# Query and key projection of a two-layer mixer: from full-precision tiles to pieces of high and low parts

## The chip, the cores and the metric

The kernel runs on one core of a Trainium2 chip. The metric is the device time of one execution in microseconds (us). One core has a matrix engine (PE, with its weight loads listed as PEld), a vector engine (DVE), a scalar engine (ACT), a general engine (POOL), and SyncE (SP), which here only issues transfers. Each engine works through its own list in order; an instruction that waits for a semaphore holds up everything behind it on that engine. On-chip memory is SBUF (128 partitions) and PSUM, eight banks of 128 x 512 words into which PE accumulates.

## What is computed

Two trunk layers over 384 tokens: 128 context tokens and 256 latent ones. Each layer projects the normalised tokens once and hands the columns to three groups:

```python
u = h @ p['w_in']                      # 1024 -> 512 + 768 + 1536 columns
y_a = conformer_group(u_a, p)          # gated, 31-tap depthwise convolution, layer norm, silu
y_b = hyena_group(u_b, p)              # two long convolutions, by spectra
q, k, v = jnp.split(u_c, 3, axis=-1)   # 512 columns each
if ang is not None:
    q = apply_axial_rope(q, ang)       # latent tokens only
    k = apply_axial_rope(k, ang)
k_all = jnp.concatenate([ctx_kv[0].astype(k.dtype), k], axis=2)   # cached keys first
o = diff_attention(q, k_all, v_all, lam)
y = jnp.concatenate([y_a, y_b, o], axis=-1) @ p['w_out']
```

After that comes a mixture of 64 experts, eight per token. All tensors are 32-bit floats.

## The kernel before

Everything is written out by hand: five engine programs, semaphores between them, and every buffer placed by hand, some over others. There is no scheduler. What orders the work is the order of each engine's list.

**The projection** of a layer is 19 tiles, which PE runs in a loop over `i` (in `block.tensor`). Tiles 0 to 9 are 128 output columns by 384 tokens, for the convolution groups. Tiles 10 to 18 are 128 tokens by 512 columns: 10 to 12 are the query's three token tiles, 13 to 15 the key's, 16 to 18 the value's. The semaphore `pe_u` counts finished tiles. Each tile goes to one of three PSUM banks, and `u_free` makes it wait until the tile three before it was read out (`u_out`, on ACT).

**Two ways of multiplying.** `u_tile` multiplies the 32-bit operands as they are; the trace records two instructions for each such product. Tiles 2 to 9 (`HALVED`) instead go by single passes: a weight piece of 128 x 1024 is rounded to a high part by ACT (`high`), its remainder, the low part, is written over the original by DVE for pieces 0 and 1 and by POOL for 2 to 7 (`RINGL` is the same memory as `RING`), and PE adds three products: high x high, low x high, high x low. The tokens are split once per layer into `HTH` and `HTL`. The high parts rotate through three buffers, two in `GROWH` and `SCRH`, so ACT's cast of one piece waits until PE has done with the piece that held the buffer (`act.wait_ge(pe_u, ...)`).

**Between the tiles** PE runs the long convolution of the hyena group, in two rounds: `z_turn` (6 transposes), `z_spectra` (18 products), and `z_conv` (12 products); each needs something from ACT or DVE in between. DVE's list in this stretch is: `gated`, `taps(0, 4)`, `z_spectra` of round 0, `taps(4, 16)`, `z_gate` of round 0, `rope` of the query, `taps(16, 24)`, `z_spectra` of round 1, `taps(24, 31)`, `conv_bias`, `rope` of the key, `z_gate` of round 1. A tap is a `scalar_tensor_tensor` over 399 columns that reads two SBUF operands, `CB` and `CA`; there are two per tap, and each waits only for the one before the last, so they run without a gap. PE's `conv_mean` waits for `conv_bias`, its `z_turn` of round 1 for `z_gate` of round 0.

**Placement** that matters: `HTH` lies under `YT`, `HTL` under the end of `KSYS`, `QT` and the first half of `KT`. `rope` keeps its four products in `RP`, which is the second half of `YT`.

**Transfers**: SP loads the query chunk `t0` after tile 3, the key chunk `t1` after tile 5, the value chunk `t2` after tile 9, then the cached keys `ck` into `KT`, and later pieces of the modulation weights and `w_out` into the slots that come free.

Of the kernel before, what the change touches and what calls it, by code (L numbers as in the profile page):

```python
# [28 lines left out]
P = 128  # L29
DM = 1024  # L30
KD = DM // P
DEPTH = 2
NT = 3
# [15 lines left out]
CHW = 4096  # L49
# [52 lines left out]
def build(nc, I, O):  # L102
    lam_init = [0.8 - 0.6 * math.exp(-0.3 * l) for l in range(DEPTH)]
    with ExitStack() as ctx:
# [12 lines left out]
        with ExitStack() as o_RINGL:  # L117
            RINGL = sb("RINGL", [P, SLOTS * CHW], F32R, c=o_RINGL)
        RING = sb("RING", [P, SLOTS * CHW])
# [122 lines left out]
        M2 = RWF[:, 1280:1792].rearrange("p (a n) -> p a n", a=2)  # L242
        ON = RWF[:, 1792:2048].rearrange("p (b n) -> p b n", b=2)

        RP = YT[:, 4:8, :].rearrange("p a b -> p (a b)")
        XN = (YT[:, :, :].rearrange("p a b -> p (a b)").rearrange("p (t d) -> p t d", t=NT),
              FLT[:, 0:NT * DM].rearrange("p (t d) -> p t d", t=NT))
        XNK = [x.rearrange("p t (q k) -> p t k q", k=KD) for x in XN]
        WHI = [GROWH[:, 0, :], GROWH[:, 1, :], SCRH[:, :]]
        HALVED = tuple(range(2, 10))  # L250
        NH3 = len(HALVED)
        FTB = ((0, 2, 4), (6, 0, 2))
        ROWB = (6, 6, 4, 6)
        COLB = (6, 5, 4, 5)
# [83 lines left out]
             "d_rope", "d_ln", "d_zs", "d_gate", "d_max", "d_P", "d_oms", "d_on", "d_x", "d_rt",  # L338
             "d_res", "d_lam"))

        a_hh, a_wh, d_hl, d_wl, p_wl = map(sem, ("a_hh", "a_wh", "d_hl", "d_wl", "p_wl"))
        p_half, p_pad, p_pow = map(sem, ("p_half", "p_pad", "p_pow"))


# [50 lines left out]

        def split_piece(l, q):

            n = ORDER[HALVED[q]]
            a, count = SLOT_OF[l, f"f{n // 4}"]
            cols = slice(a * CHW + (n % 4) * DM, a * CHW + (n % 4 + 1) * DM)  # L400
            return a, count, RING[:, cols], RINGL[:, cols], WHI[q % 3]

        HTHF = HTH[:, :, :].rearrange("p k t -> p (k t)")
        HTLF = HTL[:, :, :].rearrange("p k t -> p (k t)")
# [5 lines left out]
        def _(sp):  # L410
# [7 lines left out]
            def weight_in(l, name):  # L418

                a = SLOT_OF[l, name][0]  # L420
                if name[0] == "f":
                    i = int(name[1])
                    src = I["wfm"][l, :, i * CHW:min((i + 1) * CHW, 10 * DM)]
                elif name[0] == "t":
                    src = I["wtm"][l, int(name[1])]
                else:
                    src = I["wo"][l, int(name[1])]
                sp.dma_start(chunk[a][:, 0:src.shape[-1]], src).then_inc(chunk_in[a], 16)

            def tiles_done(l, n):  # L430
                sp.wait_ge(pe_u, 19 * l + n)
# [16 lines left out]
            for l in range(DEPTH):  # L448
# [21 lines left out]
                weight_in(l, "t1")  # L470
                tiles_done(l, 10)
                weight_in(l, "t2")
                sp.dma_start(KT[:, :, P:2 * P], I["ck"][l]).then_inc(ctx_in, 16)
                tiles_done(l, 13)
                mod_in(fill(l, 0)[0])
                tiles_done(l, 16)
                weight_in(l, "o0")
                sp.wait_ge(pe_conv, 4 * (l + 1))
                mod_in(fill(l, 1)[0])
# [171 lines left out]
        def _(pe):  # L651
# [72 lines left out]
            def z_turn(l, o):  # L724

                if o == 0:
                    pe.wait_ge(a_spec, 6 * l + 6)
                    pe.wait_ge(d_sc, K_SC * l + 12)
                else:
                    pe.wait_ge(d_gate, K_GATE * l + 4)  # L730
                for t in range(NT):
                    for c in range(2):
                        mm = nc.tensor.transpose(PS[t // 2][:, (t % 2) * 256 + c * P:(t % 2) * 256 + (c + 1) * P],
                                                 CO[:, c, t * P:(t + 1) * P], ident)
                mm.then_inc(pe_ztr, 1)
# [162 lines left out]
            def u_rest(l, i):  # L898
# [6 lines left out]
                    mm = nc.tensor.matmul(PS[3 + i % 3][:, 0:TOK], hi[:, k, :], HTL[:, k, :], start=False, stop=(k == KD - 1))  # L905
                mm.then_inc(pe_u, 1)

            def u_tile(l, i):

                n = ORDER[i]  # L910
                name = f"f{n // 4}" if n < 10 else f"t{(n - 10) // 3}"
                a, count = SLOT_OF[l, name]
                pe.wait_ge(chunk_in[a], 16 * count)
                u_free(l, i)
                if n < 10:
                    w = RING[:, a * CHW + (n % 4) * DM:a * CHW + (n % 4 + 1) * DM].rearrange("p (k f) -> p k f", k=KD)
                    for k in range(KD):
                        mm = nc.tensor.matmul(PS[3 + i % 3][:, 0:TOK], w[:, k, :], HT[:, k, :], start=(k == 0), stop=(k == KD - 1))  # L918
                else:
                    w = RING[:, a * CHW:(a + 1) * CHW].rearrange("p (k n) -> p k n", k=KD)  # L920
                    t = (n - 10) % 3
                    for k in range(KD):
                        mm = nc.tensor.matmul(PS[3 + i % 3][:, :], HT[:, k, t * P:(t + 1) * P], w[:, k, :],  # L923
                                              start=(k == 0), stop=(k == KD - 1))
                mm.then_inc(pe_u, 1)
# [223 lines left out]
            for l in range(DEPTH):  # L1149
# [15 lines left out]
                        to_features(l, 0, t)  # L1165

                features_done(l, 0, 2)
                for i in range(19):
                    if i not in HALVED:
                        u_tile(l, i)  # L1170
                    elif i == 2:
                        u_high(l, 2)
                        u_high(l, 3)
                        u_rest(l, 2)
                        u_rest(l, 3)
                    elif i > 3:
                        u_high(l, i)
                        u_rest(l, i)
                    if l > 0 and i < 2:
                        hidden(l, i)  # L1180
                    if 3 <= i < 6:
                        filters(l, i - 3)
                    if 6 <= i < 9:
                        spectra(l, i - 6)
                    if i in (9, 13):
                        z_turn(l, i // 10)
                    if i in (10, 14):
                        z_spectra(l, i // 13)
                    if i in (12, 16):
                        z_conv(l, i // 15)  # L1190
                    if i == 16:
                        conv_mean(l)
                    if i == 17:
                        conv_var(l)
                    if i >= 17:
                        for h in range(NH):
                            qk_turn(l, i - 17, h)
# [91 lines left out]
        def _(act):  # L1289
# [141 lines left out]
            def z_out(l, o):  # L1431
                act.wait_ge(pe_ztr, 2 * l + o + 1)
                if o == 0:
                    act.wait_ge(d_sc, K_SC * l + 12)
                own.sig(sc.activation(ZT[:, 0:2, :].rearrange("p t n -> p (t n)"), PS[0][:, :], ACT.Copy), a_zt)
                own.sig(sc.activation(ZT[:, 2, :], PS[1][:, 0:256], ACT.Copy), a_zt)

            def high(l, q):

                a, count, whole, low, high_ = split_piece(l, q)  # L1440
                act.wait_ge(chunk_in[a], 16 * count)
                if q == 0:
                    act.wait_ge(d_x, 6 * l)
                    act.wait_ge(pe_mod, 1)
                if q >= 3:
                    act.wait_ge(pe_u, 19 * l + HALVED[q - 3] + 1)
                sc.activation(high_, whole, ACT.Copy).then_inc(a_wh, 1)

            def u_out(l, i):
# [25 lines left out]
            for l in range(DEPTH):  # L1475
# [29 lines left out]
                high(l, 1)  # L1505

                act.wait_ge(p_pad, 6 * (l + 1))
                for i in range(19):
                    u_out(l, i)
                    if l > 0 and i < 2:  # L1510
                        hidden(l, i)
                    if 1 <= i < 7:
                        high(l, i + 1)
                    if 6 <= i < 9:
                        spectra(l, i - 6)
                    if i in (9, 13):
                        z_out(l, i // 10)
                    if i >= 17:
                        for h in range(NH):
                            qk_out(l, i - 17, h)  # L1520
# [67 lines left out]
        def _(dve):  # L1588
# [318 lines left out]

            def rope(l, c):

                for t in (1, 2):  # L1910
                    dve.wait_ge(a_u, K_AU * l + au(10 + 3 * c + t))
                    x = QKV[:, t, 512 * c:512 * (c + 1)].rearrange("p (g h s i) -> p g h s i", g=8, h=2, s=2)
                    x1, x2 = x[:, :, :, 0, :], x[:, :, :, 1, :]
                    cs = cst("cos")[:, (t - 1) * 32:t * 32].rearrange("p (h i) -> p h i", h=2).unsqueeze(1).to_broadcast([P, 8, 2, 16])
                    sn = cst("sin")[:, (t - 1) * 32:t * 32].rearrange("p (h i) -> p h i", h=2).unsqueeze(1).to_broadcast([P, 8, 2, 16])
                    T = [RP[:, j * 256:(j + 1) * 256].rearrange("p (g h i) -> p g h i", g=8, h=2) for j in range(4)]
                    own.wait(d_rope)
                    sig(v.tensor_tensor(T[0], x1, cs, ALU.mult), d_rope)
                    sig(v.tensor_tensor(T[1], x2, sn, ALU.mult), d_rope)
                    sig(v.tensor_tensor(T[2], x1, sn, ALU.mult), d_rope)  # L1920
                    sig(v.tensor_tensor(T[3], x2, cs, ALU.mult), d_rope)
                    own.wait(d_rope)
                    sig(v.tensor_tensor(x1, T[0], T[1], ALU.subtract), d_rope)
                    sig(v.tensor_tensor(x2, T[2], T[3], ALU.add), d_rope)
# [306 lines left out]
```

## Time and profile before

| | us |
|---|---|
| median of 3 runs (1756.74 to 1760.15) | 1758.61 |
| profiled execution | 1757.6 |
| its span in the trace | 1755.8 |
| PE busy, share of the span | 1666.8, 95% |
| DVE busy | 644.9, 37% |
| ACT busy | 387.0, 22% |
| POOL busy | 220.8, 13% |
| granted PE clock, mean | 0.978 |

The share of PE is an average over stages. Which engine sets the pace of one stage is seen from the idle time in that stage alone. The stretch that the change touches begins, in layer 0, at 107.5 us with `z_turn` and ends at 195.4 us with the first attention product; layer 1 has the same stretch 860.2 us later. In a row, a name such as `RING` is a buffer, and `PSB` the whole of PSUM.

### The profile page before, as it was taken

How to read it: one execution, taken by the hardware profiler on the slowest of the kernel's cores; microseconds unless marked ns; L12 is line 12 of the kernel's file. 1: busy time of each engine (PE TensorE's matmuls, PEld its weight loads, DVE VectorE, ACT ScalarE, POOL GpSimd, SP SyncE). 2: the span in 40 equal slices, each digit the busy share in tenths (PEclk: the TensorE clock that was granted, in tenths of full speed). 3: DMA queues.
4: the chain of work that ended last, by engine and by line, in shares of the span. 5: the costliest groups of instructions: out<-in, count | busy, mean ns of one | idle time of the engine just before them, and what ended most of it. 6: DMA issues, size and time to landing. Idle time of an engine off the chain costs nothing.

```text
span 1755.8 us, 22346 instructions
## 1 busy us (share of the span) xinstructions
PE 1666.8 (95%) x8468; PEld 823.9 (47%) x8468; DVE 644.9 (37%) x1709; ACT 387.0 (22%) x842; POOL 220.8 (13%) x217
## 2 busy tenths in 40 slices
PE   4999889999999999999969998999999999999996
PEld 2765344644444444444447553555444444444442
DVE  2479362422222222222165866442222222222223
ACT  2310343211111111111153114431111111111111
POOL 0200000011111111111103000001111111111110
PEclk8999999999999999999979998999999999999998
DMA  9312744399999999999732229017899999999993
GB/s 402 131 54 100 281 207 174 126 403 373 417 400 418 416 394 413 421 419 419 322 127 96 102 96 395 1 60 316 341 418 411 408 419 393 414 419 419 420 419 126
DMA packets 77291, 530.52 MB, mean 302 GB/s; under 512 B 10880, under 2 KB 14080, under 8 KB 21632
## 3 DMA queue, kind: packets, MB, share of 16 engines
q1 hardware_dynamic: 67392, 503.90, 70.3%
q0 software_dynamic: 9792, 25.18, 3.7%
q8 instruction: 69, 1.13, 0.3%
q14 instruction: 38, 0.31, 0.0%
HBM read 533.76 MB, written 5.77 MB: 307 GB/s over the span
## 4 chain that ended last, share of the span: by engine, by line
PE 90%; DVE 4%; DMA 2%; ACT 2%; issue 1%; SPq 0%; ACTq 0%; POOL 0%; DVEq 0%
PE PSB L931 30%; PE PSB L940 15%; PE PSB L923 7%; PE PSB L985 6%; PE PSB L986 5%; PE PSB L973 4%; PE PSB L859 4%; DMA RING<-in_wmod 2%; PE PSB L679 1%; PE PSB L918 1%; PE PSB L895 1%; PE PSB L958 1%; PE PSB L905 1%; PE PSB L896 1%; PE PSB L947 1%
## 5 line engine op out<-in xcount | busy, mean ns | idle before, releaser
L931 PE MATMUL PSB<-WB,EX 128*32 128x512 f32 (+2 forms) x1408 | 431.9, 598 | 0.0
L931 PE MATMUL PSB<-RING,EX 128*32 128x512 f32 (+2 forms) x1344 | 417.1, 598 | 1.7 <-DVE EX L1770 1.7
L940 PE MATMUL PSB<-RING,AT 128*32 128x512 f32 (+2 forms) x720 | 226.7, 597 | 4.8 <-ACT GROW L1298 3.7
L1788 DVE TENSOR_TENSOR YL<-PSB,YH 128x512 fp32r<-128x512 f32 x136 | 94.1, 692 | 353.7 <-ACT YH L1377 353.7
L940 PE MATMUL PSB<-WB,AT 128*32 128x512 f32 (+2 forms) x704 | 210.8, 596 | 0.0
L563 POOL TENSOR_SCALAR SCAT<-CST,LSTT 128x384 fp32r<-128x384 f32 x68 | 84.9, 1248 | 833.1 <-PE PSB L986 833.0
L931 PEld LDWEIGHTS PSB<-WB,EX 128*32 128x32 f32 (+2 forms) x1408 | 113.0, 126 | 135.7 <-issue 135.7
L985 PE MATMUL PSB<-YH,SCAT 128*128 128x512 f32 x408 | 171.7, 421 | 2.8 <-DVE YL L1788 2.8
L931 PEld LDWEIGHTS PSB<-RING,EX 128*32 128x32 f32 (+2 forms) x1344 | 105.8, 124 | 122.5 <-issue 122.5
L1770 DVE COPY EX<-PSB 128x512 f32<-128x512 f32 x68 | 47.1, 692 | 315.7 <-PE PSB L973 315.7
L986 PE MATMUL PSB<-YL,SCAT 128*128 128x512 f32 x408 | 161.0, 395 | 0.0
L1377 ACT ACTIVATE YH<-PSB 128x512 fp32r<-128x512 f32 x136 | 81.2, 597 | 239.6 <-PE PSB L940 239.6
L923 PE MATMUL PSB<-RING,HT 128*128 128x512 f32 x288 | 125.9, 592 | 0.0
L973 PEld LDWEIGHTS PSB<-CST,XG 128*128 128x128 f32 x544 | 58.5, 141 | 106.6 <-issue 104.8
L940 PEld LDWEIGHTS PSB<-RING,AT 128*32 128x32 f32 (+2 forms) x720 | 62.5, 129 | 78.1 <-issue 74.2
L1370 ACT ACTIVATE SGM<-PSB 128x256 f32<-128x256 f32 x68 | 26.1, 383 | 311.9 <-PE PSB L931 311.9
L940 PEld LDWEIGHTS PSB<-WB,AT 128*32 128x32 f32 (+2 forms) x704 | 58.4, 126 | 72.5 <-issue 72.0
L973 PE MATMUL PSB<-CST,XG 128*128 128x128 f32 x544 | 88.2, 285 | 1.4 <-ACT EX L1352 1.4
L555 POOL DMA_INDIRECT XG<-h_rows,IDX x68 | 74.5, 1096 | 113.4 <-DVE LSTW L1740 91.2
L985 PEld LDWEIGHTS PSB<-YH,SCAT 128*128 128x128 f32 x408 | 77.6, 190 | 21.1 <-issue 4.9
L859 PE MATMUL PSB<-RING,YT 128*128 128x512 f32 x192 | 86.5, 598 | 0.0
L923 PEld LDWEIGHTS PSB<-RING,HT 128*128 128x128 f32 x288 | 54.3, 190 | 63.0 <-issue 62.2
(282 smaller groups left out, 1867.9 us busy)
## 6 DMA issues: line engine op xcount, KB each, us to landing
RING<-in_exp_w_gate SPq DMA_DIRECT2D x64, 1024.0 KB, 12.3
RING<-in_exp_w_up SPq DMA_DIRECT2D x64, 1024.0 KB, 14.4
RING<-in_exp_w_down SPq DMA_DIRECT2D x64, 1024.0 KB, 12.8
WB<-in_exp_w_gate SPq DMA_DIRECT2D x64, 1024.0 KB, 10.1
WB<-in_exp_w_up SPq DMA_DIRECT2D x64, 1024.0 KB, 13.6
WB<-in_exp_w_down SPq DMA_DIRECT2D x64, 1024.0 KB, 13.3
RING<-in_wmod SPq DMA_DIRECT2D x16, 2048.0 KB, 10.4
KSYS<-in_wmod SPq DMA_DIRECT2D x8, 2048.0 KB, 11.6
```

The costliest lines, as they stand in the source:

```text
L555: pool.indirect_dma_start(XG[:, s % 2, :], None, h_rows, bass.IndirectOffsetOnAxis(ap=IDX[:, s:s + 1], axis=0), bounds_check=TOK - 1, oob_ ...
L563: nc.gpsimd.tensor_scalar(SCAT[:, s % 2, :], cst("iota"), LSTT[:, s:s + 1], None, ALU.is_equal).then_inc(p_scat, 1)
L859: mm = nc.tensor.matmul(PS[YB[0][t] + hf][:, :], YT[:, f, t * P:(t + 1) * P], w[:, f, :], start=(f == 0), stop=(f == 7))
L923: mm = nc.tensor.matmul(PS[3 + i % 3][:, :], HT[:, k, t * P:(t + 1) * P], w[:, k, :], start=(k == 0), stop=(k == KD - 1))
L931: mm = nc.tensor.matmul(PS[6][s0:s0 + w, :].rearrange("p (w f) -> p w f", w=2), e[:, k, s0:s0 + w], rawgu[n % NBUF][:, k], start=(k == 0), ...
L940: mm = nc.tensor.matmul(dst[s0:s0 + w, :], AT[:, j, s0:s0 + w], rawdn[n % NBUF][:, hf, j], start=(j == 0), stop=(j == 1))
L973: mm = nc.tensor.transpose(PS[7][:, c * P:(c + 1) * P], XG[:, s % 2, k * P:(k + 1) * P], ident)
L985: nc.tensor.matmul(PS[piece][:, :], w, YHb[s % 2][:, cols], start=False, stop=False, skip_group_check=True)
L986: mm = nc.tensor.matmul(PS[piece][:, :], w, YLb[s % 2][:, cols], start=False, stop=True, skip_group_check=True)
L1377: sc.activation(YHb[s % 2][:, hf * 512:(hf + 1) * 512], PS[6 + hf][:, :], ACT.Copy).then_inc(a_yh, 1)
L1770: v.tensor_copy(EX2[:, s % 2, 4:8, :].rearrange("p k s -> p (k s)"), PS[7][:, :]).then_inc(e_high, 1)
L1788: v.tensor_tensor(YLb[s % 2][:, hf * 512:(hf + 1) * 512], PS[6 + hf][:, :], YHb[s % 2][:, hf * 512:(hf + 1) * 512].bitcast(F32), ALU.subtr ...
```

## The change

The query and key tiles (10 to 15) leave `u_tile`. Each of their two chunks (128 x 4096 weights) is cut into four pieces of two contraction blocks, 128 x 1024 each. ACT rounds a piece to its high part, POOL writes the low part over the original, and PE (`qk_piece`) takes the piece for all three token tiles at once: for two blocks and three tiles, three products each, 18 in all. So a chunk's three tiles stay open in three banks and are finished in its last piece. The eight new pieces use only the two `GROWH` buffers in turn; ACT's cast waits for the piece two before it, by the new semaphore `pe_wk` (or `pe_u` at the end of a chunk).

PE's list is written out again around them: `z_turn` 0, piece 0, `z_spectra` 0, pieces 1 to 3, `z_conv` 0, piece 4, `z_turn` 1, piece 5, `z_spectra` 1, pieces 6 and 7, then the value tiles as before. ACT's and POOL's lists get the casts and the subtractions. DVE's list keeps its order. `RP` moves from `YT` to `SCR` (over `SCRH`), and `rope` waits for tile 7. Since `HTH` and `HTL` now live until tile 15, the cached keys, which land over `HTL`, are loaded after tile 15 instead of behind `t2`.

```diff
-        RP = YT[:, 4:8, :].rearrange("p a b -> p (a b)")
+        RP = SCR[:, 0:DM]
-        NH3 = len(HALVED)
+        NFM, NH3 = len(HALVED), len(HALVED) + 8
         def split_piece(l, q):
+            if q < NFM:
+                n = ORDER[HALVED[q]]
+                name, part, high = f"f{n // 4}", n % 4, WHI[q % 3]
+            else:
+                c, part = divmod(q - NFM, 4)
+                name, high = f"t{c}", WHI[q % 2]
...
-                sp.dma_start(KT[:, :, P:2 * P], I["ck"][l]).then_inc(ctx_in, 16)
                 tiles_done(l, 13)
                 mod_in(fill(l, 0)[0])
                 tiles_done(l, 16)
+                sp.dma_start(KT[:, :, P:2 * P], I["ck"][l]).then_inc(ctx_in, 16)
                 weight_in(l, "o0")
...
+            def qk_piece(l, c, j):
+                q = NFM + 4 * c + j
+                a, count, whole, low, high = split_piece(l, q)
+                pe.wait_ge(p_wl, (NH3 - 2) * l + q - 1)
+                hi = high.rearrange("p (k n) -> p k n", k=2)
+                lo = low.rearrange("p (k n) -> p k n", k=2)
+                for kk in range(2):
+                    k = 2 * j + kk
+                    for t in range(NT):
+                        i = 10 + 3 * c + t
+                        if k == 0:
+                            u_free(l, i)
+                        dst = PS[3 + i % 3][:, :]
+                        ht, hl = HTH[:, k, t * P:(t + 1) * P], HTL[:, k, t * P:(t + 1) * P]
+                        nc.tensor.matmul(dst, ht, hi[:, kk, :], start=(k == 0), stop=False)
+                        nc.tensor.matmul(dst, ht, lo[:, kk, :], start=False, stop=False)
+                        mm = nc.tensor.matmul(dst, hl, hi[:, kk, :], start=False, stop=(k == KD - 1))
+                        if k == KD - 1:
+                            mm.then_inc(pe_u, 1)
+                if j < 3:
+                    mm.then_inc(pe_wk, 1)
...
-                if q >= 3:
+                if 3 <= q < NFM:
                     act.wait_ge(pe_u, 19 * l + HALVED[q - 3] + 1)
+                elif NFM <= q < NFM + 2:
+                    act.wait_ge(pe_u, 19 * l + HALVED[q - 2] + 1)
+                elif q == NFM + 5:
+                    act.wait_ge(pe_u, 19 * l + 13)
+                elif q >= NFM + 2:
+                    act.wait_ge(pe_wk, 6 * l + q - NFM - 1 - (1 if q > NFM + 5 else 0))
                 sc.activation(high_, whole, ACT.Copy).then_inc(a_wh, 1)
...
             def rope(l, c):
+                dve.wait_ge(pe_u, 19 * l + 8)
```

PE in layer 0 before, from the first transposes of the long convolution (L733) to its spectra (L745, L749) and the query tiles (L923, each row of one and seven is a tile):

```order
L733 MATMUL PSB<-CST,CO 128x128 [waits d_sc,a_spec]
L733 MATMUL PSB<-CST,CO 128x128 x5
L923 MATMUL PSB<-RING,HT 128x512 [waits a_u,chunk_in0]
L923 MATMUL PSB<-RING,HT 128x512 x7
L745 MATMUL PSB<-RW,CST 128x256 [waits a_zt]
L745 MATMUL PSB<-RW,CST 128x256
L749 MATMUL PSB<-RW,CST 128x256 x8
L923 MATMUL PSB<-RING,HT 128x512 [waits d_u,chunk_in0]
```

PE at the same place in the change; L738 is the transposes, L750 and L754 the spectra, L928 to L930 the three products of one block and token tile:

```order
L738 MATMUL PSB<-CST,CO 128x128 [waits d_sc,a_spec]
L738 MATMUL PSB<-CST,CO 128x128 x5
L928 MATMUL PSB<-GROWH,HTH 128x512 [waits a_u,p_wl]
L929 MATMUL PSB<-RINGL,HTH 128x512
L930 MATMUL PSB<-GROWH,HTL 128x512
...
L750 MATMUL PSB<-RW,CST 128x256 [waits a_zt]
L750 MATMUL PSB<-RW,CST 128x256
L754 MATMUL PSB<-RW,CST 128x256 x8
L928 MATMUL PSB<-GROWH,HTH 128x512 [waits p_wl]
```

A tile's wait for its chunk (`chunk_in0`) has become a piece's wait for POOL's low part (`p_wl`), and one piece stands between the transposes and the spectra where a whole tile stood.

ACT before, from the sigmoid of tile 9 (L1457) over the read-outs of `z_turn` (L1435, L1436) and of the projection tiles (L1463):

```order
L1457 ACTIVATE SG<-PSB 128x384 [waits pe_u]
L1435 ACTIVATE RW<-PSB 128x512 [waits d_sc,pe_ztr]
L1436 ACTIVATE RW<-PSB 128x256
L1463 ACTIVATE QKV<-PSB 128x512 [waits pe_u] x4
L1435 ACTIVATE RW<-PSB 128x512 [waits pe_ztr]
L1436 ACTIVATE RW<-PSB 128x256
```

ACT in the change, with the casts to the high part as L1492 and the read-outs as L1474, L1475 and L1508:

```order
L1492 ACTIVATE GROWH<-RING 128x1024 [waits pe_u,chunk_in0]
L1502 ACTIVATE SG<-PSB 128x384 [waits pe_u]
L1474 ACTIVATE RW<-PSB 128x512 [waits d_sc,pe_ztr]
L1475 ACTIVATE RW<-PSB 128x256
L1492 ACTIVATE GROWH<-RING 128x1024 [waits pe_u,chunk_in0]
L1492 ACTIVATE GROWH<-RING 128x1024 [waits pe_wk,chunk_in0] x2
L1492 ACTIVATE GROWH<-RING 128x1024 [waits pe_wk,chunk_in2]
L1508 ACTIVATE QKV<-PSB 128x512 [waits pe_u] x3
L1492 ACTIVATE GROWH<-RING 128x1024 [waits pe_u,chunk_in2]
L1474 ACTIVATE RW<-PSB 128x512 [waits pe_ztr]
L1475 ACTIVATE RW<-PSB 128x256
L1492 ACTIVATE GROWH<-RING 128x1024 [waits pe_wk,chunk_in2] x2
```

The eight casts stand among the read-outs, and the second `z_turn` is read out between the sixth and the seventh of them.

## Rows read from the trace of the kernel before

**Rows 1.** Windows, both layers: length; busy of PE, PEld, DVE, ACT, POOL; clock.

```profile
107.50:195.00 87.50, 86.44 (x286) 48.59 (x283) 62.81 (x127) 10.98 (x26) 0.86 (x1) 1.00 0.28 103
968.00:1055.00 87.00, 86.16 (x284) 48.34 (x281) 62.82 (x127) 10.70 (x25) 0.86 (x1) 1.00 0.28 103
```

**Rows 2.** Timeline of PE in that stretch, layer 0: start, length, operation, count.

```profile
108.18 7.03 PE L923 MATMUL PSB<-RING,HT 128*128 128x512 f32 x16
115.05 1.03 PE L745 MATMUL PSB<-RW,CST 128*128 128x256 f32 x4
...
119.36 13.90 PE L923 MATMUL PSB<-RING,HT 128*128 128x512 f32 x32
133.09 0.61 PE L759 MATMUL PSB<-CST,KSYS 128*128 128x128 f32 x4
...
137.44 7.03 PE L923 MATMUL PSB<-RING,HT 128*128 128x512 f32 x16
...
174.23 1.45 PE L772 MATMUL PSB<-CB,CST 128*128 128x384 f32 x4
```

**Rows 3.** Timeline of PE in an expert step: single-pass products of 512 columns.

```profile
414.28 0.40 PE L986 MATMUL PSB<-YL,SCAT 128*128 128x512 f32 x1
...
415.66 0.40 PE L986 MATMUL PSB<-YL,SCAT 128*128 128x512 f32 x1
```

**Rows 4.** Timeline of ACT, one cast, and line L633, POOL's subtractions: min/median/max ns.

```profile
66.71 1.06 ACT L1447 ACTIVATE GROWH<-RING 128x1024 fp32r<-128x1024 f32 x1
...
L633 POOL TENSOR_TENSOR RINGL<-RING,GROWH x8: 2360/2397/3828, 67.8 to 948.0; 128x1024 fp32r<-128x1024 f32 x8
```

**Rows 5.** Timelines of DVE and POOL around 70 us, layer 0.

```profile
69.65 0.69 DVE L1856 TENSOR_TENSOR QKV<-PSB,CST 128x512 f32<-128x512 f32 x1 [15.67 <-PE PSB L702]
70.97 2.15 DVE L1858 TENSOR_TENSOR QKV<-QKV 128x512 f32<-128x512 f32 x1
...
67.85 4.72 POOL L633 TENSOR_TENSOR RINGL<-RING,GROWH 128x1024 fp32r<-128x1024 f32 x2 [4.52 <-ACT GROWH L1447]
```

**Rows 6.** Timelines of DVE and POOL around 88 us, and POOL's twin in layer 1.

```profile
86.62 2.72 DVE L1876 SCALAR_TENSOR_TENSOR CO<-RW,PR,CO 128x128 f32<-128x128 f32 x8
89.38 3.20 DVE L1873 TENSOR_SCALAR CO<-RW,PR 128x128 f32<-128x128 f32 x4
...
87.76 3.83 POOL L633 TENSOR_TENSOR RINGL<-RING,GROWH 128x1024 fp32r<-128x1024 f32 x1 [3.50 <-ACT GROWH L1447]
...
947.97 3.83 POOL L633 TENSOR_TENSOR RINGL<-RING,GROWH 128x1024 fp32r<-128x1024 f32 x1 [3.50 <-ACT GROWH L1447]
```

**Rows 7.** Timeline of DVE in the touched stretch, layer 0.

```profile
116.11 0.69 DVE L1945 TENSOR_TENSOR RW<-PSB,KSYS 128x512 f32<-128x512 f32 x1 [3.10 <-PE PSB L745]
...
122.48 13.17 DVE L1898 SCALAR_TENSOR_TENSOR CA<-CB,PR,CA 128x399 f32<-128x399 f32 x24
...
137.64 0.61 DVE L1956 SCALAR_TENSOR_TENSOR CO<-CO,PR,PSB 128x384 f32<-128x384 f32 x1 [0.87 <-PE PSB L764]
...
143.36 8.81 DVE L1898 SCALAR_TENSOR_TENSOR CA<-CB,PR,CA 128x399 f32<-128x399 f32 x16
...
167.02 1.03 DVE L1905 TENSOR_TENSOR CB<-CA,PR 128x256 f32<-128x256 f32 x2
```

**Rows 8.** Timeline of PE and windows of 1 us behind a pause, attention of layer 0.

```profile
228.79 0.55 PE L1220 MATMUL PSB<-CST,HT 128*128 128x128 f32 x3 [2.00 <-DVE HT L2064]
...
229.00:230.00 1.00, 1.00 (x7) 0.30 (x9) 0.90 (x4) 0.54 (x2) 0.55 (x1) 0.66 0.96 410
230.00:231.00 1.00, 1.00 (x12) 0.24 (x8) 0.93 (x3) 0.95 (x3) 0.00 (x0) 0.50 0.97 410
231.00:232.00 1.00, 1.00 (x12) 0.18 (x4) 0.93 (x3) 0.86 (x3) 0.00 (x0) 0.50 1.11 475
232.00:233.00 1.00, 1.00 (x9) 0.19 (x2) 1.00 (x1) 0.04 (x1) 0.00 (x0) 0.64 0.95 393
```

**Rows 9.** Transfers: KB each, median us from issue to landing.

```profile
KT<-in_ck SPq DMA_DIRECT2D x2, 256.0 KB, 8.3
```

More of the change, by code:

```diff
@@ L339, in build @@
              "d_res", "d_lam"))
-        a_hh, a_wh, d_hl, d_wl, p_wl = map(sem, ("a_hh", "a_wh", "d_hl", "d_wl", "p_wl"))
+        a_hh, a_wh, d_hl, d_wl, p_wl, pe_wk = map(sem, ("a_hh", "a_wh", "d_hl", "d_wl", "p_wl", "pe_wk"))
         p_half, p_pad, p_pow = map(sem, ("p_half", "p_pad", "p_pow"))
@@ L396, in split_piece @@
         def split_piece(l, q):
[L398 to L401, printed above, removed]
+            if q < NFM:
[4 more added lines that the diff above has]
+                name, high = f"t{c}", WHI[q % 2]
+            a, count = SLOT_OF[l, name]
+            cols = slice(a * CHW + part * DM, a * CHW + (part + 1) * DM)
+            return a, count, RING[:, cols], RINGL[:, cols], high
         HTHF = HTH[:, :, :].rearrange("p k t -> p (k t)")
@@ L1167, in _ @@
                 features_done(l, 0, 2)
-                for i in range(19):
+                for i in range(10):
                     if i not in HALVED:
@@ L1184, in _ @@
                         spectra(l, i - 6)
[L1185 to L1190, printed above, removed]
+                z_turn(l, 0)
+                qk_piece(l, 0, 0)
+                z_spectra(l, 0)
+                qk_piece(l, 0, 1)
+                qk_piece(l, 0, 2)
+                qk_piece(l, 0, 3)
+                z_conv(l, 0)
+                qk_piece(l, 1, 0)
+                z_turn(l, 1)
+                qk_piece(l, 1, 1)
+                z_spectra(l, 1)
+                qk_piece(l, 1, 2)
+                qk_piece(l, 1, 3)
+                for i in range(16, 19):
+                    u_tile(l, i)
+                    if i == 16:
+                        z_conv(l, 1)
                     if i == 16:
@@ L1507, in _ @@
                 act.wait_ge(p_pad, 6 * (l + 1))
-                for i in range(19):
+                for i in range(10):
                     u_out(l, i)
@@ L1515, in _ @@
                         spectra(l, i - 6)
-                    if i in (9, 13):
-                        z_out(l, i // 10)
+                    if i == 8:
+                        high(l, 8)
+                z_out(l, 0)
+                for q in range(9, 13):
+                    high(l, q)
+                for i in range(10, 13):
+                    u_out(l, i)
+                high(l, 13)
+                z_out(l, 1)
+                high(l, 14)
+                high(l, 15)
+                for i in range(13, 19):
+                    u_out(l, i)
                     if i >= 17:
```

## The prediction

> **What bounds the kernel now.** I read the windows first. In the touched stretch PE is busy for 86.4 of 87.5 us at full clock, in both layers, and POOL does next to nothing there (0.86 us) [rows 1]. DVE is busy for 62.8 us. So PE sets the pace, and work taken off PE counts in full as long as nothing else gets in front. Then the timeline of PE, for what a tile and each piece of the long convolution cost [rows 2]; then the timelines of ACT, POOL and DVE, for what the new pieces will wait for [rows 4 to 7]. The sum is made against the profiled execution (1757.6 us, of which 1755.8 are the span); it lies 1.0 us below the median of the runs.
>
> **PE's own work.** Two query tiles take 13.73 us (119.36 to 133.09) [rows 2], so a tile takes 6.87 and six take 41.2. The new form has 8 pieces of 18 single-pass products. In the expert step such a product of 512 columns starts every 0.23 us (415.66 less 414.28, over six) [rows 3], so a piece takes 4.14 and eight take 33.1: **8.1 us less per layer**. The cast on ACT is 1.06 us, POOL's subtraction 2.40 [rows 4]; eight of each are 8.5 and 19.2 us per layer, on engines that are busy for 11.0 and 0.9 us in the stretch [rows 1]. By this count alone a piece's preparation (0.2 us from PE to ACT, 1.06, 0.1, 2.40, 0.1: 3.9 us) just fits behind one piece of PE, and POOL would hide it.
>
> **What POOL's subtraction meets.** It does not run freely beside DVE. At 70.97 a DVE operation with two SBUF operands, whose equal behind it took 0.68, took 2.15 and ended 0.55 after POOL's; one with a PSUM operand at 69.65 took its usual 0.69 under POOL [rows 5]. The other way round: at 87.76 POOL's subtraction was released while DVE was 1.1 us into a run of eight `scalar_tensor_tensor` of two SBUF operands. It took 3.83 instead of 2.40, that is 1.43 more, and ended at 91.59, so its own 2.40 began at 89.19, just where that run ended (86.62 + 2.72); the run lost nothing, and DVE's next group of four took 3.20. Layer 1 repeats it to the hundredth [rows 6]. So POOL does not get in between two such instructions while the run goes on; it waits for the run's end, and then DVE waits for POOL.
>
> The Trainium skill (SBUF — State Buffer, section "Who interferes with whom") says that a DVE instruction with two SBUF inputs contends with a GpSimd instruction that reads SBUF, and that whoever issues first has the shared ports for that whole instruction while the other fully blocks. For POOL behind DVE the rule read by itself would let POOL in after one instruction of about 0.55 us, which would make the first rival below, 1769, out of what I forecast as 1780; the trace agrees with the blocking (2.15 for 0.68) and shows a wait of four further instructions and not of one.
>
> The taps are exactly such runs, longer ones: 24 in 13.17 us, and 16 in 8.81 [rows 7]. Whether POOL starves for 24 of them the trace does not show; the bounds are 0 (no wait), 0.55 (one tap) and the whole rest of the run. I take the whole rest, by the nearest row.
>
> **The new order in layer 0, step by step.** PE runs piece 0 from 108.3 to 112.4, `z_spectra` (4.31 us, 115.05 to 119.36 [rows 2]) to 116.8, pieces 1 and 2 to 125.0. DVE's first spectra operation came 1.06 us behind PE's (116.11 against 115.05), and the group lasted 6.37 until the taps at 122.48 [rows 2, 7]. Now it starts at 113.5. The low parts of pieces 1 and 2 fall before and into it: the former waits behind the first taps until 112.9, and the two hold up DVE's two-operand steps by 0.5 and 1.0. So the 24 taps start at 121.2 and end at 134.3.
>
> **First new wait.** The cast for piece 3 is released when piece 1 ends (120.9), and POOL is asked for its low part at 122.3, over a microsecond into the run. It gets the memory at 134.3, and the piece is ready at 136.8. PE has been free since 125.0: **11.8 us**. Behind the waiting piece stand `z_conv`, and behind that DVE's `z_gate`, the query's `rope` and all that follows; ACT's reads of tiles 10 to 12 also wait.
>
> **Second new wait.** Piece 3 ends at 142.6 (with the slow clock below), `z_conv` (4.35 us, 133.09 to 137.44 [rows 2]) at 147.0, pieces 4 and 5 with the transposes between them at 155.9, `z_spectra` at 160.2. ACT casts piece 6 behind the read-out of those transposes and asks POOL at 153.9. DVE, after `z_gate`, a wait of 1.3 behind piece 5's low part, and `rope` (4.4), began its run of 16 taps at 152.9 and leaves at 161.6. The piece is ready at 164.1: **3.9 us**. Piece 7's low part is ready while PE works on piece 6.
>
> **The clock.** After 2.0 us without work PE went to half its clock, from 2.4 to 1.2 GHz, for some 3 us: over four windows the granted clock was 0.66, 0.50, 0.50 and 0.64, which lost 1.7 us [rows 8]. Both new waits are longer: 2 x 1.7 = **3.4 us**.
>
> **At no cost.** `rope`'s wait for tile 7 is over some 40 us before `rope` runs. `RP` in `SCR` changes no length. The later `ck` lands in 8.3 us [rows 9]; from tile 15 to the first attention product there are over 30 us, with the value tiles in them. On SP it stands ahead of `o0`, under the same wait for tile 15, and delays that by about a microsecond; `o0` is first used in step 9 of attention. Without that cover it would be 8.3 us per layer.
>
> **Sum per layer**: -8.1 + 11.8 + 3.9 + 3.4 = +11.0. Layer 1 has the same stretch at the same offsets [rows 1], so 22 in all: 1757.6 + 22 = 1779.6, **1780 us**.
>
> **Rivals.** *POOL gets in after the tap that is running* (each engine then waits for one instruction of the other). No wait of PE for a low part remains, but DVE becomes the bound: its list from the first spectra operation to the end of `conv_bias` ran from 116.11 to 168.05 with about 1 us idle [rows 7], 51 us; six subtractions of 2.40 now fall into it, 14.4. From 113.5 that ends at 179, and `conv_mean`, which waits for it, stood at 174.23 [rows 2]: +4.7, and one loss of clock, 1.7 (the second is inside DVE's time). About +6 per layer: 1769. For it: a fair lock is the simpler mechanism. Against it: rows 6, twice.
>
> *POOL and DVE do not hinder each other here* (the side of faster): then the 8.1 us come in full, 1757.6 - 16.2 = 1741. This needs POOL to read beside the taps; it decides as soon as POOL's subtraction ends within about 4 us of its cast in the 24 taps. Rows 5 and 6 speak against it, and only a difference between the taps and the group at 86.62 would rescue it.
>
> *The order comes out otherwise by a microsecond or two*: if the fourth low part is released before the spectra group's last step, it goes ahead of the taps and the run is pushed behind by 2.4; the fifth then waits in its place. I put that between the first rival and the forecast, 1769 to 1777.
>
> **How the numbers follow.** Forecast as reckoned, 0.60 (own range 1775 to 1786: a subtraction of 2.4 to 2.8, a loss of clock of 1.4 to 2.2, a third wait of PE). Turn by turn, or order changed, 0.24. No hindrance, 0.13. Something else, mostly near no change, 0.03. The range leaves out the last two: 1764 to 1787. A difference under 0.2% (3.5 us) cannot be told from none here. Faster 0.13, same 0.03, slower 0.84.
>
> **What would show it.** In the profile after: PE idle of about 12 us before the fourth piece and 4 before the seventh, released by POOL; a POOL subtraction of about 14 us beside 24 unhindered taps (13.2 us), and another of about 10 beside the 16; PE busy some 16 us less, 0.23 us per product; granted clock below 1 behind the waits. Wrong if POOL's subtractions stay near 2.4 us under the taps, if the 24 taps grow by multiples of 2.4 (the first rival), or if the stretch of each layer gets shorter.

## The result and the profile after

The changed kernel takes 1765.36 us (median of 8 runs, 1762.35 to 1767.81) against 1757.2 beside it (8 runs, 1750.88 to 1760.15): a ratio of 1.005, with a 95% interval of 1.0038 to 1.0062. It is slower by 8 us where 22 were forecast. The profiled execution took 1767.81 us, of which 1766.0 are the span.

Windows of the same stretch as in [rows 1], of the changed kernel (length; busy of PE, PEld, DVE, ACT, POOL; granted clock, DMA share, GB/s):

```profile
107.50:195.00 87.50, 78.89 (x317) 57.27 (x316) 76.97 (x127) 15.84 (x24) 19.02 (x9) 0.94 0.26 99
968.00:1055.00 87.00, 78.67 (x326) 59.17 (x325) 76.96 (x127) 16.12 (x23) 20.17 (x9) 0.94 0.27 100
```

PE is busy for 78.9 us instead of 86.4, as wanted. But DVE is now busy for 77.0 instead of 62.8, with the same 127 instructions. The timeline of POOL, all eight new subtractions of layer 0 (start, length; in brackets the idle time before):

```profile
105.47 2.39 POOL L638 TENSOR_TENSOR RINGL<-RING,GROWH 128x1024 fp32r<-128x1024 f32 x1 [14.07 <-ACT GROWH L1492]
110.08 2.80 POOL L638 TENSOR_TENSOR RINGL<-RING,GROWH 128x1024 fp32r<-128x1024 f32 x1 [2.22 <-ACT GROWH L1492]
113.78 2.35 POOL L638 TENSOR_TENSOR RINGL<-RING,GROWH 128x1024 fp32r<-128x1024 f32 x1 [0.89 <-ACT GROWH L1492]
122.28 2.40 POOL L638 TENSOR_TENSOR RINGL<-RING,GROWH 128x1024 fp32r<-128x1024 f32 x1 [6.15 <-ACT GROWH L1492]
126.45 2.73 POOL L638 TENSOR_TENSOR RINGL<-RING,GROWH 128x1024 fp32r<-128x1024 f32 x1 [1.78 <-ACT GROWH L1492]
131.05 2.41 POOL L638 TENSOR_TENSOR RINGL<-RING,GROWH 128x1024 fp32r<-128x1024 f32 x1 [1.87 <-ACT GROWH L1492]
148.39 2.49 POOL L638 TENSOR_TENSOR RINGL<-RING,GROWH 128x1024 fp32r<-128x1024 f32 x1 [14.92 <-ACT GROWH L1492]
153.82 2.62 POOL L638 TENSOR_TENSOR RINGL<-RING,GROWH 128x1024 fp32r<-128x1024 f32 x1 [2.94 <-ACT GROWH L1492]
```

None starves: the longest is 2.80, 0.4 us above the bare 2.40, less than one tap. What they take, DVE loses. The timeline of DVE, its runs of taps (6, 24 and 16 instructions; compare [rows 7]):

```profile
109.46 7.64 DVE L1954 SCALAR_TENSOR_TENSOR CA<-CB,PR,CA 128x399 f32<-128x399 f32 x6
...
125.22 17.41 DVE L1954 SCALAR_TENSOR_TENSOR CA<-CB,PR,CA 128x399 f32<-128x399 f32 x24
...
144.30 0.56 DVE L2015 TENSOR_TENSOR CO<-CO 128x384 f32<-128x384 f32 x1
...
151.42 10.91 DVE L1954 SCALAR_TENSOR_TENSOR CA<-CB,PR,CA 128x399 f32<-128x399 f32 x16
```

The 24 taps took 13.17 before, the 16 took 8.81: 4.2 and 2.1 more, 2.1 us for each subtraction that falls into the run. So the second transposes of PE wait for DVE's `z_gate` (L2015), and the mean for `conv_bias` (L1961), behind DVE's last taps. PE's waits in 107.5 to 205 (us in total, times, longest), its timeline, and a window behind the first wait:

```profile
PE PSB L738 <- DVE CO L2015: 7.0, 1, 7.0
PE PSB L777 <- DVE CB L1961: 1.0, 1, 1.0
...
144.92 1.54 PE L738 MATMUL PSB<-CST,CO 128*128 128x128 f32 x6 [6.99 <-DVE CO L2015]
...
199.35 0.49 PE L1250 MATMUL PSB<-KT,QT 64*128 64x128 f32 x4 [0.69 <-issue]
...
145.00:150.00 5.00, 5.00 (x15) 4.23 (x16) 4.83 (x11) 1.82 (x3) 1.61 (x1) 0.50 0.01 2
```

After 7.0 us without work, PE ran another 5 us at a granted clock of 0.50, that is 1.2 GHz, and lost about 2.5 us there. The first product of attention stands at 199.35 instead of 195.36 (the line that is L1211 in the kernel before): 4.0 us late. In layer 1 the same stretch grew from 87.8 to 92.0 us. Two layers make some 8 us, as much as the medians differ. The two profiled executions are 10.2 us apart; the other 2 lie outside the stretch, and their cause is not shown.

### The profile page after: what moved, and what is told of

Its sections match the earlier page's. It is cut to its first block, busy times and chain, and to the rows that moved or that the text cites. A ratio compares the mean times of both kernels' runs of the same rounds, so it can differ in the third digit from the quotient of the medians.

```text
span 1766.0 us, 22579 instructions
## 1 busy us (share of the span) xinstructions
PE 1660.1 (94%) x8564; PEld 845.6 (48%) x8564; DVE 673.2 (38%) x1709; ACT 403.1 (23%) x858; POOL 261.5 (15%) x233
## 4 chain that ended last, share of the span: by engine, by line
PE 81%; DVE 13%; DMA 2%; ACT 2%; issue 1%; SPq 0%; ACTq 0%; POOL 0%; DVEq 0%
PE PSB L959 30%; PE PSB L968 15%; PE PSB L1013 6%; PE PSB L1014 5%; DVE CA L1954 5%; PE PSB L1001 4%; PE PSB L864 4%; DMA RING<-in_wmod 2%; PE PSB L684 2%; PE PSB L946 1%; PE PSB L900 1%; PE PSB L986 1%; PE PSB L910 1%; PE PSB L901 1%; PE PSB L975 1%
## 5 line engine op out<-in xcount | busy, mean ns | idle before, releaser
L1954 DVE SCALAR_TENSOR_TENSOR CA<-CB,PR,CA 128x399 f32<-128x399 f32 x120 | 87.3, 802 | 0.0
L1014 PEld LDWEIGHTS PSB<-YL,SCAT 128*128 128x128 f32 x408 | 77.1, 189 | 12.1
```

Of the source, the lines that this page charges most:

```text
L1014: mm = nc.tensor.matmul(PS[piece][:, :], w, YLb[s % 2][:, cols], start=False, stop=True, skip_group_check=True)
L1954: sig(v.scalar_tensor_tensor(out=CA[:, c, :], in0=src, scalar=cw[:, c, w:w + 1], in1=CA[:, c, :], op0=ALU.mult, op1=ALU.add), d_cv)
```

## The experiments

The changed kernel's time, 1765.4, is the one to compare with. The kernel before ran beside each group of runs, at 1754.9 to 1756.3.

**Take POOL's reads away.** POOL writes zeros where it made the eight low parts.

```diff
-  nc.gpsimd.tensor_tensor(rest, whole, high.bitcast(F32), ALU.subtract).then_inc(p_wl, 1)
+  if q < NFM:
+      nc.gpsimd.tensor_tensor(rest, whole, high.bitcast(F32), ALU.subtract).then_inc(p_wl, 1)
+  else:
+      nc.gpsimd.memset(rest.bitcast(F32), 0.0).then_inc(p_wl, 1)
```

> The changed kernel, but for the eight new pieces GpSimd writes zeros instead of the low part (it leaves out the low-part products' values; the products themselves run as before), so it no longer reads SBUF beside the taps. Theory (the price of the change is the turn-by-turn memory of DVE and GpSimd): the taps return from a mean of 802 ns to about 632, the wait of 7.0 us of PE before the second transposes (L738 at 144.9) and the one before conv_mean fall, and the time goes to 1741 to 1746 us. Rival (the new order of PE, its chain cast - low part - piece and the clock cost it by themselves): no more than 3 us faster than the changed kernel, 1762 to 1768. If writing alone also holds DVE up, the taps stay above 700 ns.

Measured: 1742.04 us (1741.43 to 1747.07), ratio to the kernel before 0.993 (0.9911 to 0.9948). The groups of DVE in 107.5 to 205 (busy us, mean ns), and the timelines of POOL and PE, of this run:

```profile
L1957 DVE SCALAR_TENSOR_TENSOR CA<-CB,PR,CA 128x399 f32<-128x399 f32 x60 | 33.1, 631 | 0.0
...
125.74 0.96 POOL L641 MEMSET RINGL<- 128x1024 f32 x1 [3.23 <-ACT GROWH L1495]
...
106.64 0.82 PE L741 MATMUL PSB<-CST,CO 128*128 128x128 f32 x6
...
186.91 0.49 PE L1253 MATMUL PSB<-KT,QT 64*128 64x128 f32 x4 [0.69 <-issue]
```

and the same group of the changed kernel:

```profile
L1954 DVE SCALAR_TENSOR_TENSOR CA<-CB,PR,CA 128x399 f32<-128x399 f32 x60 | 43.7, 803 | 0.0
```

and of the kernel before:

```profile
L1898 DVE SCALAR_TENSOR_TENSOR CA<-CB,PR,CA 128x399 f32<-128x399 f32 x60 | 33.0, 631 | 0.0
```

The taps are back at 631 ns with POOL writing beside them, and PE's waits for DVE are gone. So the price of the change is POOL's reading, 23 us over both layers (1765.4 less 1742.0), and the new order of PE costs nothing by itself: the rival falls. The zeros are also ready sooner (0.96 us instead of 2.40), but that is not the gain: in the changed kernel PE has no wait for a low part. From the first transposes to attention it is 80.3 us here (106.64 to 186.91) and was 87.8 before (107.52 to 195.36): PE's own gain is 7.6 per layer, near the 8.1 reckoned.

**Give the low parts to DVE, with and without a later mean.** DVE makes seven of the eight low parts at chosen places in its list; in the first run below `conv_mean` and `conv_var` also stand one tile later on PE, and DVE's `z_gate` of round 1 stands ahead of the last twelve taps instead of at the end of the list. The core of the edit:

```diff
-                for q in range(2, NH3):          # POOL
+                for q in range(2, NFM + 1):
...
-                taps(0, 4)                       # DVE
-                z_spectra(l, 0)
-                taps(4, 16)
+                taps(0, 1)
+                low(l, 9)
+                taps(1, 3)
+                z_spectra(l, 0, 10)              # low(l, 10) ahead of its third tile
+                taps(3, 5)
+                low(l, 11)
+                taps(5, 9)
+                low(l, 12)
+                taps(9, 11)
                 z_gate(l, 0)
+                low(l, 13)
...
-                taps(16, 24)
-                z_spectra(l, 1)
-                taps(24, CW)
+                low(l, 14)
+                taps(11, 13)
+                z_spectra(l, 1, 15)
+                taps(13, 25)                     # 13 to CW in the second run,
+                z_gate(l, 1)                     # with z_gate at the end as before
+                taps(25, CW)
                 conv_bias()
                 rope(l, 1)
-                z_gate(l, 1)
...
-                    if i == 16:                  # PE, first run only
-                        conv_mean(l)
-                    if i == 17:
+                    if i == 18:
                         conv_var(l)
...
+                    if i == 17:
+                        conv_mean(l)
```

> The changed kernel with the low parts of the last seven pieces made by DVE at chosen places between its taps (1.22 us each, 8.5 us per layer, in place of seven turns of GpSimd of about 2.4 us, 17 us of DVE's time), conv_mean and conv_var one tile later on PE. Theory (DVE is the bound, and GpSimd's turns are what it lost): DVE's list is some 8 us shorter, PE keeps most of the 8.1 us per layer, 1742 to 1748 us. Rival (the order of PE or the clock is the cause, not DVE's time): 1760 or more.

> As the run e2_dve_low_late_mean, but conv_mean, conv_var and the last z_gate stay where the changed kernel has them. It parts what e2 gained (1741.8) into the low parts on DVE and the later mean. If GpSimd's turns are nearly all of the loss, DVE's list is about 8 us per layer shorter than in the changed kernel, and conv_mean then waits for DVE by only a few us: 1748 to 1756. If the later mean was what helped, this stays near the changed kernel, 1762 to 1767.

Measured: 1741.84 us (1741.12 to 1744.16), ratio 0.992 (0.9906 to 0.9933), with the later mean and the earlier `z_gate`; 1760.29 (1758.82 to 1760.86), ratio 1.0025 (1.0014 to 1.0037), without them, 4 us above what was expected. The groups of DVE in 107.5 to 205, a wait of PE, the first `qk_turn` (L807), and attention's start, in the run with the later mean:

```profile
L1957 DVE SCALAR_TENSOR_TENSOR CA<-CB,PR,CA 128x399 f32<-128x399 f32 x60 | 33.3, 627 | 0.0
L1990 DVE TENSOR_TENSOR RINGL<-RING,GROWH 128x1024 fp32r<-128x1024 f32 x7 | 8.5, 1221 | 0.5 <-ACT GROWH L1495 0.5
...
PE PSB L777 <- DVE CB L1964: 0.2, 1, 0.2
...
172.60 0.82 PE L807 MATMUL PSB<-CST,QKV 128*128 128x128 f32 x6
...
187.29 0.49 PE L1253 MATMUL PSB<-KT,QT 64*128 64x128 f32 x4 [0.69 <-issue]
```

The timeline of PE and a window in the run without them:

```profile
172.12 2.93 PE L777 MATMUL PSB<-CB,CST 128*128 128x384 f32 x4 [5.46 <-DVE CB L1964]
...
173.00:176.00 3.00, 3.00 (x6) 1.57 (x5) 2.83 (x9) 0.00 (x0) 0.00 (x0) 0.50 0.03 11
```

DVE makes a low part in 1.22 us, where POOL takes 2.40 and holds DVE up for some 2.1 meanwhile. That alone leaves a wait of 5.5 us before the mean, and half clock behind it (0.50 over 3 us); with the other two edits 0.2 us of wait is left. This version beats both kernels. The earlier `z_gate` has a part in it: PE's first `qk_turn` waits for it, and stands at 172.60, while DVE's list up to the key's `rope` ends at 179.3. At the end of that list `z_gate` would have held PE up by some 6 us (an estimate from these two times). No run tries it apart.

**The later mean alone**, POOL making the low parts (the same PE edit, nothing else).

> The changed kernel with conv_mean and conv_var one tile later on PE and nothing else; GpSimd makes the low parts as before. The low parts on DVE without the later mean gave 1760.3, with it 1741.8; this run is the other half. If the two losses of the changed kernel are in a row on DVE's list (the wait of 7.0 us before the second transposes, and the one of 1.0 before conv_mean), the later mean here takes away only the second and its like: 1761 to 1766. Rival (the later mean is itself most of the gain): 1750 or less.

Measured: 1760.27 us (1758.41 to 1763.55), ratio 1.0024 (1.0015 to 1.0034), 0.7 us below what was expected. PE's waits in the stretch:

```profile
PE PSB L738 <- DVE CO L2015: 7.0, 1, 7.0
PE PSB L807 <- DVE YT L2015: 1.4, 1, 1.4
```

The large wait stays, the one before the mean is gone, and one of 1.4 for the last `z_gate` (now before the first `qk_turn`) has come. So either edit alone is worth 5 us in the medians (1765.4 less 1760.3), and both with the earlier `z_gate` 24 (less 1741.8). In the profiles the stretch from the transposes to attention, 92.0 us in the changed kernel's layer 0, takes 91.0 with the later mean, 88.9 with the low parts on DVE, and 80.7 with all three. The rest of the later mean's 5 us is not explained. Only the run with all three edits takes DVE off the path.

**Why did POOL starve at 88 us and not in the taps?** In [rows 6] it waited for the end of a run of short instructions, released three ahead; the taps are longer, and released one ahead. Two runs with each tap in two halves:

```diff
-                    for c in range(2):
+                    for c, a0, a1 in ((0, 0, 200), (0, 200, CAW), (1, 0, 200), (1, 200, CAW)):
...
-                            own.wait(d_cv, 1)
+                            own.wait(d_cv, 3)    # ahead by three; by one in the other run
```

> The changed kernel with each tap in two halves (200 and 199 columns, four chains) released three instructions ahead instead of one. It tells why GpSimd starved in the group at 86.6 us (3.83 us for 2.40) and not in the taps. Depth theory (GpSimd gets in only when DVE's next instruction isn't released yet): GpSimd's subtractions in the taps now take the rest of the run, 4 us or more, and the run of 24 taps is not lengthened within. Length theory (short instructions alone do it): the same here, and also in the other kernel with halves released one ahead. If neither counts: subtractions of 2.4 to 2.8 as in the changed kernel.

> The changed kernel with each tap in two halves (200 and 199 columns), released one instruction ahead as now, and the short convolution, too, released one ahead instead of three. Depth theory: GpSimd's subtractions stay at 2.4 to 2.8 us in the taps, and the one at 87.8 us, 3.83 until now, falls to 2.4 to 2.9. Length theory: subtractions of 4 us or more in the taps, and 3.8 again at 87.8.

Measured, one run each: 1781.1 and 1777.65 us. The timelines of POOL (layers 0 and 1) and DVE with halves released one ahead:

```profile
88.09 3.83 POOL L638 TENSOR_TENSOR RINGL<-RING,GROWH 128x1024 fp32r<-128x1024 f32 x1 [3.50 <-ACT GROWH L1492]
...
126.97 2.47 POOL L638 TENSOR_TENSOR RINGL<-RING,GROWH 128x1024 fp32r<-128x1024 f32 x1 [1.76 <-ACT GROWH L1492]
131.57 14.80 POOL L638 TENSOR_TENSOR RINGL<-RING,GROWH 128x1024 fp32r<-128x1024 f32 x1 [2.13 <-ACT GROWH L1492]
...
1004.17 2.63 POOL L638 TENSOR_TENSOR RINGL<-RING,GROWH 128x1024 fp32r<-128x1024 f32 x1 [2.16 <-ACT GROWH L1492]
...
125.75 18.42 DVE L1954 SCALAR_TENSOR_TENSOR CA<-CB,PR,CA 128x200 f32<-128x200 f32 x48
```

Here is the starving that was forecast: 14.80 us, to the end of the run at 144.1. It comes with one ahead as with three (14.79 there), so the depth theory falls. But length alone doesn't say it either: at 126.97 POOL got in at once, 1.2 us after the run began. The requests at 131.57 and, in layer 1, at 1004.17 came both 2.1 us after POOL's last turn, at the same place, and went opposite ways. Beside the 16 taps the eighth piece starved in both layers (10.86 and 10.56 us). That how long DVE has run may count is a guess at this point.

**Ask later in a run of whole taps.** POOL is held back by small memsets of a buffer of its own.

```diff
+                    for _ in range({NFM + 4: 16, NFM + 7: 20}.get(q, 0)):
+                        own.do(nc.gpsimd.memset(DLY[:, :], 0.0), p_dl)
                     nc.gpsimd.tensor_tensor(rest, whole, high.bitcast(F32), ALU.subtract).then_inc(p_wl, 1)
```

> The changed kernel with GpSimd held back by small memsets of its own buffer (16 and 20 of 128 columns) ahead of the low parts of the fifth and the eighth new piece, so that it asks for the memory several whole taps later in DVE's uninterrupted run, as it did where the half taps starved it (6 instructions into the run). If a run that has gone on for some time shuts GpSimd out whatever its instructions' length, one of these two subtractions takes the rest of its run, 5 us or more. If the length of the instruction counts, both stay at 2.4 to 3.0 us, however late they ask. The time is later than the changed kernel's by the waits of PE that the holding back makes, some 2 to 8 us.

Measured, one run: 1761.68 us. The timelines of POOL and DVE, and PE's waits:

```profile
129.71 9.92 POOL L641 TENSOR_TENSOR RINGL<-RING,GROWH 128x1024 fp32r<-128x1024 f32 x1
...
124.25 13.16 DVE L1957 SCALAR_TENSOR_TENSOR CA<-CB,PR,CA 128x399 f32<-128x399 f32 x24
...
PE PSB L931 <- POOL RINGL L641: 7.6, 2, 6.9
```

POOL asked ten taps into the run (129.71 less 124.25, at 0.55 each) and starved to its end; the 24 taps took 13.16, undisturbed. So whole taps do it as well: how far the run has gone decides. The time was expected above the changed kernel's and came out, in one run, 4 us below its median: PE now waits 6.9 us for the low part instead of 7.0 for DVE, and DVE, not held up, has no wait before the mean.

**Where the limit lies**: the same with 6 and 8 memsets (layers 0 and 1), then 10 and 12, ahead of the fifth piece alone.

> The changed kernel with GpSimd held back by small memsets before the fifth piece only: 6 in layer 0 and 8 in layer 1, so that it asks when DVE has run some 5 (layer 0) and 6 (layer 1) whole taps since its last pause. Count theory: 2.4 to 3.0 us with 5; with 6, where the half taps went either way, open. Rival (only the length of the run that is left, or the instruction's length, decides): both starve to the run's end (over 10 us), or neither does.

> The same with 10 memsets in layer 0 and 12 in layer 1, for 7 and 8 whole taps since the last pause. Count theory: both wait for the end of the run of 24 taps, 10 to 12 us. Rival (time since the pause, of more than about 4 us, decides, or the instruction's length): 2.4 to 3.0 us in one or both.

Measured, one run each: 1766.8 and 1765.52 us. The timelines of POOL and DVE with 6 and 8:

```profile
128.56 2.77 POOL L641 TENSOR_TENSOR RINGL<-RING,GROWH 128x1024 fp32r<-128x1024 f32 x1
...
125.74 17.39 DVE L1957 SCALAR_TENSOR_TENSOR CA<-CB,PR,CA 128x399 f32<-128x399 f32 x24
...
994.78 12.03 POOL L641 TENSOR_TENSOR RINGL<-RING,GROWH 128x1024 fp32r<-128x1024 f32 x1
...
991.43 13.16 DVE L1957 SCALAR_TENSOR_TENSOR CA<-CB,PR,CA 128x399 f32<-128x399 f32 x24
```

and of POOL with 10 and 12:

```profile
128.64 11.50 POOL L641 TENSOR_TENSOR RINGL<-RING,GROWH 128x1024 fp32r<-128x1024 f32 x1
...
994.86 10.97 POOL L641 TENSOR_TENSOR RINGL<-RING,GROWH 128x1024 fp32r<-128x1024 f32 x1
```

Asked 2.82 us into the run (five taps done) POOL is let in; at 3.35 us (six) it waits for the end, and so at seven and eight. The operation just ahead of the taps counts too, since DVE does not pause between them; the one ahead of that, which POOL's last turn had held up, is left out. Counted so, POOL was let in after six instructions without a pause, shut out after seven, eight and nine. In [rows 6] it was shut out after seven (four `tensor_scalar` with one SBUF operand, three others), at 2.3 us; counting operations with two SBUF operands alone would leave three there, and not fit. Time does not order these cases (let in at 2.82, shut out at 2.3, and at 2.1 with halves), the count nearly does: after five the halves were shut out in three cases of four, and whole taps were let in, so with five or six it went either way.

**Put a pause into the run.** Two runs: half taps, each released when the one before has ended, in the short convolution too; and the run with 16 and 20 memsets, with DVE waiting once in every eight whole taps.

```diff
-                            own.wait(d_cv, 1)
+                            own.wait(d_cv)       # halves; also d_sc in the short convolution
...
+                            own.wait(d_cv, 0 if w % 4 == 0 and c == 0 else 1)    # whole taps
```

> Half taps as in the two runs before, but each released only when the one before it has ended, in the taps and in the short convolution. If GpSimd gets in wherever DVE pauses between two instructions, no subtraction takes more than 3 us, the one at 87.8 us included, at the price of a pause per instruction (the taps' mean above 0.34 us per half). If the instruction's length alone counts, the subtractions beside the later taps still take 8 us or more, and the one at 87.8 us 3.8.

> As the run e6_deep_in_run, where GpSimd asked some ten whole taps into an unbroken run of DVE and waited 7.5 us for its end, but DVE now waits before every eighth tap (every fourth pair) for the one before it to end, a pause of about 0.1 us. Count theory (GpSimd gets in while DVE has run fewer than about six instructions since its last pause): the low part of the fifth piece, asked two or three taps behind such a pause, takes 2.4 to 3.0 us in both layers, and the 24 taps grow from 13.2 to about 15.6 or 18. Rival (it was the late time or the held-back GpSimd itself): it again takes 5 us or more.

Measured, one run each: 1812.77 and 1768.12 us. The timelines of POOL and DVE in the run with all halves in series:

```profile
87.01 2.49 POOL L638 TENSOR_TENSOR RINGL<-RING,GROWH 128x1024 fp32r<-128x1024 f32 x1 [3.50 <-ACT GROWH L1492]
...
128.83 24.11 DVE L1954 SCALAR_TENSOR_TENSOR CA<-CB,PR,CA 128x200 f32<-128x200 f32 x48
```

and with a pause in every eight taps:

```profile
129.61 2.42 POOL L641 TENSOR_TENSOR RINGL<-RING,GROWH 128x1024 fp32r<-128x1024 f32 x1
...
124.17 17.64 DVE L1957 SCALAR_TENSOR_TENSOR CA<-CB,PR,CA 128x399 f32<-128x399 f32 x24
```

In series no subtraction of the two stretches took over 2.6, and the one at 88 us fell from 3.83 to 2.49. With a pause two taps ahead of the request, the same request that took 9.92 took 2.42, and in layer 1 as well. So a pause of DVE lets POOL in where an unbroken run shuts it out.

## Why the prediction was wrong

- **PE's own work**: right. 8.1 us per layer were reckoned, 7.6 measured.
- **The step that failed**: "I take the whole rest, by the nearest row." The nearest row [rows 6] showed POOL shut out after seven instructions without a pause; in the changed kernel it asks at most five instructions after one (counted as above), and each of its own turns makes the next pause. It never has to wait for more than the tap that is running. So the first new wait (11.8) and the second (3.9) for a low part do not exist, and the first rival holds, which I put at 0.24 with the other order: DVE pays. The time lies inside the range of 1764 to 1787 only because that was drawn wide enough for this rival; it does not speak for the forecast.
- **The order**: the fourth low part was asked for at 122.28, as reckoned (122.3), but DVE's 24 taps began at 125.22 and not at 121.2. POOL's turns there had cost DVE some 2 us each (six taps took 7.64, at 0.55 each they are 3.3), where 0.5 and 1.0 were reckoned. So this low part went ahead of the taps, which is the condition of the third rival. A starving POOL would have made PE wait before the fifth piece, as in the run with 16 and 20 memsets, not before the fourth.
- **The rival's size**: about +6 per layer reckoned, 4.0 measured. The working of it put the loss at `conv_mean` (+4.7) and one loss of clock; in the trace 7.0 of 8.4 us of wait stand earlier, at the second transposes, since the `z_gate` in front of them is behind 24 taps that took 17.4. Gain 7.6, waits 7.0, 1.0 and 0.4, and some 2.5 to 3 of clock (1.7 was reckoned) make +3.3 to +3.8.
- **The price of starving**, too, was set too high. Where it was brought about in whole taps, PE waited 6.9 us and not 11.8, and the kernel was not seen to be slower than the changed one (1761.7 and 1765.5 in single runs): while POOL waits, DVE's taps go on undisturbed.
- **The rule read by itself**: the Trainium skill (SBUF — State Buffer, section "Who interferes with whom") has whoever issues first hold the shared ports for that whole instruction. Taken at its word, one instruction at a time, it gave the first rival, and the eight subtractions of the changed kernel agree (2.35 to 2.80). The requests deep in an unbroken run do not (9.92 to 12.03): there the measurement decides. I set the rule aside for one row, repeated in both layers, of another run of instructions. The same section says that a GpSimd instruction which only writes does not contend; the run with zeros agrees (631 ns per tap under the writes, 631 before).
- **At no cost**: `rope`'s wait, `RP` in `SCR` and the later `ck` show no wait in the trace, as reckoned.

## What to carry to other kernels

A helper engine whose reads hold the busy one up is not free because it is idle: count its turns as time of the engine that it holds up, and ask whether that engine could not do the work itself (1.22 us against 2.40 here). Before a wait seen in one place is carried to another, ask what came just before it in both places; two rows that repeat in two layers are one observation. And when the bound moves to another engine, shortening its list and moving what waits for it go together: either alone gave 5 us here, both 24, with `z_gate` moved as well.

## What was not expected of the hardware

POOL, asking for operands in SBUF beside a run of DVE instructions with two SBUF operands, got in at the end of the running one (waits up to 0.41 us) while DVE had done up to four without a pause, and waited for the end of the run in every case once it had done seven or more (the instruction that POOL itself had held up left out); between the two it went both ways (2.77 us in all after six, 14.80 after five halves). A pause of about 0.12 us between two instructions is enough (halves in series start every 0.46 us instead of 0.34: 24.11 and 18.42, each less one turn of 2.1, over 48) to let it in. What in the chip makes the count is not shown here.
